# Computing only the 64 changed columns in each level of a triangular inverse, with level 0 turned by transposes

## Chip, cores and metric

The program runs on one core of one Trainium2 chip, written directly against the engines: TensorE (PE; its weight loads are shown apart as PEld), VectorE (DVE), ScalarE (ACT), GpSimd (POOL) and SyncE (SP, which only issues transfers). The metric is the device time of one execution in microseconds (us); lower is better.

## The reference

Three transformer blocks on one sequence of 256 tokens, width 1024, all in float32. The change lies in the first block, in its RWKV-7 mixer: 8 heads of width 64, with a recurrence over the tokens.

```python
def rwkv7_scan(r, w, k, v, a_vec, b_vec):
    def step(state, inp):
        rt, wt, kt, vt, at, bt = inp
        sa = jnp.einsum('bhvk,bhk->bhv', state, at)
        state = state * wt[:, :, None, :] + sa[..., None] * bt[:, :, None, :] + vt[..., None] * kt[:, :, None, :]
        return state, jnp.einsum('bhvk,bhk->bhv', state, rt)
    s0 = jnp.zeros((B, H, N, N), jnp.float32)
    _, y = lax.scan(step, s0, (tm(r), tm(w), tm(k), tm(v), tm(a_vec), tm(b_vec)))
    return y.transpose(1, 0, 2, 3)
```

The kernel doesn't step through the tokens. It cuts them into two chunks of 128. Within a chunk the terms `sa` solve a triangular system of 128 unknowns per head, so for each of the 16 pairs of chunk and head it forms a strictly triangular 128x128 matrix A and builds the inverse of (1 - A).

## The kernel before

**The inverse.** The 16 matrices stand side by side in `AAB` (128 partitions, 16 x 128 columns) and are worked in four groups `g` of four. There are seven levels `lv`. Level `lv` joins diagonal blocks of 2^lv rows to blocks of twice the size: a mask `lvl{lv}` picks from A the blocks that connect the halves of each pair (into `ALA`, by POOL). `TI` and `TJ` hold the inverse so far and its transpose. With level 0 both are set up (unit matrix plus the masked part). Each later level makes three products of 128x128 matrices for each of the 16 matrices:

- P = ALA^T TI (line 1091), which ACT copies from the accumulator to SBUF, tile `PP` (line 1118);
- J = PP^T TJ (line 1102), which DVE adds to `TJ` (line 1152);
- I = TJ^T PP (line 1109), which DVE adds to `TI` (line 1150; not in level 6).

Level 0 has one product, with the unit matrix as moving operand, which only turns `ALA` over (line 1091 too; lines 1141 and 1143 are DVE's two operations behind it). A float32 product is two instructions of PE in the trace, so 16 products are 32 rows of MATMUL. A transpose in PE's transpose mode (line 462) is one.

**Order.** PE runs a level as: P for groups 0 to 3, then for each group J and I. The groups' other work (POOL's mask, ACT's copy, DVE's additions) goes on beside it. Every engine has its own program in a fixed order. `wait_ge(*at(step))` waits for a named step of another engine, `up(...)` signals one, `bank(e, use)` takes one of the eight accumulator banks (`ps`) in turn and waits until its last use is freed.

**Around it.** Before the inverse PE makes the matrices A (`pe_mats`, line 1055) while DVE masks them (`dve_mats`, line 1064, 64 operations). In levels 2 and 3 DVE also does four operations of `dve_bonus` (lines 1126 to 1134). Behind the inverse `pe_recurrences` goes on with the decays of the linear attention (line 1283), the first chunk's right sides (line 1165: 128x64 moving columns), and further products of 64 columns (lines 1181, 1190, 1193), some over only 64 partitions (lines 1170, 1196, 1328).

**Memory.** `PP` stands in an area (`mats + 4096`) that earlier holds weights of the input projections. `mats + 6144` belongs to the same area and isn't used by the inverse.

Of the kernel before, what the change touches and what calls it, by code (L numbers as in the profile page):

```python
# [187 lines left out]
def program(nc, a):  # L188
    ctx = ExitStack()
    with ctx:  # L190
# [456 lines left out]
        LA = SIG  # L647
        mats = ARENA - 8192
        AAB = place(mats, 16, 128)
        PP = place(mats + 4096, 16, 128)  # L650
        AAK = place(ee + 2048, 16, 128)
        ARB = place(ee + 4096, 16, 128)
        ARK = place(mats + 2048, 16, 128)
# [10 lines left out]
        def group(x, g):  # L664
            return x[:, 4 * g:4 * g + 4, :]
# [4 lines left out]
        def four(use):  # L670
            return ps(use).rearrange("p (s t) -> p s t", s=4)
# [393 lines left out]
                k.then_inc(*up("masked", use, ("free", use)))  # L1065


        def pool_inverse(e):
            for lv in range(7):
                for g in range(NG):  # L1070
                    if lv == 0:
                        e.wait_ge(*at(("m", 4 * g + 3)))
                        if g == 0:
                            e.wait_ge(*at(("bt", 3)))
                            e.wait_ge(*at(("la", 1)))
                    else:
                        e.wait_ge(*at(("p done", lv - 1, g)))
                        if lv == 1:
                            e.wait_ge(*at(("tj", 0, g)))
                    e.tensor_tensor(group(ALA, g), group(AAB, g), bc(f"lvl{lv}"), ALU.mult).then_inc(  # L1080
                        *up("level", ("al", lv, g)))

        def pe_inverse(e):
            for lv in range(7):
                for g in range(NG):
                    b = bank(e, ("p", lv, g))
                    e.wait_ge(*at(("al", lv, g)))
                    if lv > 0:
                        e.wait_ge(*at(("ti", lv - 1, g)))
                    for s in range(4):  # L1090
                        k = e.matmul(b[:, s * P:s * P + P], ALA[:, 4 * g + s, :],  # L1091
                                     ident if lv == 0 else TI[:, 4 * g + s, :], start=True, stop=True)
                    k.then_inc(*up("inverse", ("p done", lv, g), ("full", ("p", lv, g))))
                if lv == 0:
                    continue
                for g in range(NG):
                    b = bank(e, ("j", lv, g))
                    e.wait_ge(*at(("pp", lv, g)))
                    if g == NG - 1:
                        e.wait_ge(*at(("tj", lv - 1, g)))  # L1100
                    for s in range(4):
                        k = e.matmul(b[:, s * P:s * P + P], group(PP, g)[:, s, :], TJ[:, 4 * g + s, :],  # L1102
                                     start=True, stop=True)
                    if lv == 6:
                        k.then_inc(*up("inverse", ("full", ("j", lv, g))))
                        continue
                    b = bank(e, ("i", lv, g))
                    for s in range(4):
                        k = e.matmul(b[:, s * P:s * P + P], TJ[:, 4 * g + s, :], group(PP, g)[:, s, :],  # L1109
                                     start=True, stop=True)  # L1110
                    k.then_inc(*up("inverse", ("full", ("i", lv, g)), ("full", ("j", lv, g))))

        def act_inverse(e):
            for lv in range(1, 7):
                for g in range(NG):
                    e.wait_ge(*at(("full", ("p", lv, g))))
                    e.wait_ge(*at(("tj", lv - 1, g)))
                    e.activation(group(PP, g), four(("p", lv, g)), ACT.Copy).then_inc(
                        *up("levels", ("pp", lv, g), ("free", ("p", lv, g))))

        def dve_bonus(e, t):
            if t == 0:
# [13 lines left out]
        def dve_inverse(e):  # L1136
            for g in range(NG):
                if g == 0:
                    e.wait_ge(*at(("kb", 1)))
                e.wait_ge(*at(("full", ("p", 0, g))))  # L1140
                e.tensor_tensor(group(TI, g), four(("p", 0, g)), bc("ident"), ALU.add).then_inc(
                    *up("tij", ("ti", 0, g), ("free", ("p", 0, g))))
                e.tensor_tensor(group(TJ, g), group(ALA, g), bc("ident"), ALU.add).then_inc(*up("tij", ("tj", 0, g)))
            for lv in range(1, 7):
                if lv in (2, 3):
                    dve_bonus(e, lv - 2)
                for g in range(NG):
                    e.wait_ge(*at(("full", ("j", lv, g))))
                    if lv < 6:
                        e.tensor_tensor(flat(group(TI, g)), ps(("i", lv, g)), flat(group(TI, g)), ALU.add).then_inc(  # L1150
                            *up("tij", ("ti", lv, g), ("free", ("i", lv, g))))
                    e.tensor_tensor(flat(group(TJ, g)), ps(("j", lv, g)), flat(group(TJ, g)), ALU.add).then_inc(
                        *up("tij", ("tj", lv, g), ("free", ("j", lv, g))))


        def pe_chunk(e, step):
# [1243 lines left out]
```

## Time and profile before

| | |
|---|---|
| median of 3 runs | 1299.88 us (1299.66 to 1301.49) |
| the profiled execution's own time | 1296.61 us |
| its span, from first to last instruction | 1294.6 us |
| PE / PEld busy | 1168.1 us (90%) / 1015.6 us (78%) |
| DVE / ACT / POOL busy | 749.6 / 524.1 / 120.8 us |
| TensorE clock granted, mean over the span | 0.905 of full |

The profiled execution is 3.3 us below the median of the runs; 2.0 us of its own time lie outside the span. The granted clock has two levels in the trace, 1.0 (2.4 GHz) and 0.5 (1.2 GHz). A stretch with a value between holds some of both. Busy time of PE counts an instruction from its start to its modelled end, so it says how long PE was occupied and not how much it computed. The time that an instruction takes in a stream is read from start to start.

### The profile page before, as it was taken

To read this page: it belongs to the slowest core of one execution; us is meant where nothing else is said; L and a number is where in the kernel's file an instruction comes from. 1 tells how busy PE (TensorE), PEld (TensorE's weight loads), DVE (VectorE), ACT (ScalarE), POOL (GpSimd) and SP (SyncE) were. 2 spreads that over 40 slices of the span, in tenths; PEclk is the share of its full clock that TensorE was granted. 3 is DMA by queue.
4 is the path that set the end of the run, shared out by engine and by line. 5 is a ranking of instruction groups with operands and counts; after the bars stand their busy time and mean duration, and the time that the engine had idled before them with its cause. 6 is when DMAs were issued, how large, how long until landed. Compare 5 with 4: busy or idle time off the path is not lost.

```text
span 1294.6 us, 17496 instructions
## 1 busy us (share of the span) xinstructions
PE 1168.1 (90%) x7196; PEld 1015.6 (78%) x7196; DVE 749.6 (58%) x1126; ACT 524.1 (40%) x742; POOL 120.8 (9%) x115
## 2 busy tenths in 40 slices
PE   5989799988799999779897993999699996999998
PEld 5788699876799988567666993998597555999885
DVE  3475685356676675746766742765653445666443
ACT  4443322023444343425664332443354344655331
POOL 0004354120300000300004000000100000000000
PEclk9899799768799999889997996999899568999999
DMA  9244000014587686234213889877253004565540
GB/s 287 85 150 153 1 2 1 1 33 163 186 269 261 228 288 240 99 122 155 98 34 121 302 165 278 274 261 262 94 170 124 0 2 130 163 195 180 205 169 32
DMA packets 112271, 193.69 MB, mean 150 GB/s; under 512 B 4514, under 2 KB 84913, under 8 KB 112066
## 3 DMA queue, kind: packets, MB, share of 16 engines
q1 hardware_dynamic: 108530, 179.65, 41.5%
q0 software_dynamic: 3248, 11.83, 4.1%
q8 instruction: 57, 0.93, 0.3%
q10 hardware_dynamic: 416, 1.11, 0.2%
q14 instruction: 20, 0.16, 0.0%
HBM read 188.38 MB, written 4.19 MB: 149 GB/s over the span
## 4 chain that ended last, share of the span: by engine, by line
PE 81%; DVE 9%; ACT 4%; DMA 3%; issue 2%; SPq 1%; POOL 0%; ACTq 0%; DVEq 0%
PE ps L399 20%; PE ps L400 20%; PE ps L401 20%; PE ps L1862 3%; PE ps L1845 3%; DMA ring<-in_ffn_w_gate_up_dram 3%; PE ps L1091 2%; PE ps L1837 2%; PE ps L1102 2%; DVE XL L532 1%; PE ps L1109 1%; DVE ARR L383 1%; PE ps L1328 1%; DVE AR L1064 1%; DVE STAT L549 1%
## 5 line engine op out<-in xcount | busy, mean ns | idle before, releaser
L383 DVE TENSOR_TENSOR ARR<-ring,ARR 128x2048 fp32r<-128x2048 f32 (+1 forms) x147 | 329.4, 2247 | 237.7 <-ACT ARR L372 237.5
L399 PE MATMUL ps<-XH,ARR 128*128 128x256 f32 x1232 | 355.8, 289 | 40.7 <-DVE ARR L383 21.0
L372 ACT ACTIVATE ARR<-ring 128x2048 fp32r<-128x2048 f32 (+1 forms) x147 | 274.8, 1877 | 249.3 <-PE ps L401 163.3
L400 PE MATMUL ps<-XL,ARR 128*128 128x256 f32 x1232 | 352.9, 286 | 0.0
L401 PE MATMUL ps<-XH,ARR 128*128 128x256 f32 x1232 | 352.5, 286 | 0.0
L399 PEld LDWEIGHTS ps<-XH,ARR 128*128 128x128 f32 x1232 | 239.4, 194 | 45.3 <-issue 38.9
L400 PEld LDWEIGHTS ps<-XL,ARR 128*128 128x128 f32 x1232 | 239.7, 195 | 0.0
L401 PEld LDWEIGHTS ps<-XH,ARR 128*128 128x128 f32 x1232 | 239.3, 194 | 0.0
L399 PE MATMUL ps<-ARR 128*128 128x512 f32 x388 | 157.3, 406 | 9.4 <-DVE ARR L484 5.8
L400 PE MATMUL ps<-ARR 128*128 128x512 f32 x388 | 155.4, 401 | 0.0
L401 PE MATMUL ps<-ARR 128*128 128x512 f32 x388 | 155.1, 400 | 0.0
L399 PEld LDWEIGHTS ps<-ARR 128*128 128x128 f32 x388 | 74.4, 192 | 31.0 <-DVE ARR L383 7.8
L401 PEld LDWEIGHTS ps<-ARR 128*128 128x128 f32 x388 | 74.4, 192 | 17.8
L400 PEld LDWEIGHTS ps<-ARR 128*128 128x128 f32 x388 | 74.5, 192 | 17.6 <-issue 0.5
L399 PE MATMUL ps<-ARR,XH 128*128 128x512 f32 (+1 forms) x160 | 62.4, 390 | 5.3 <-DVE XL L532 3.8
L400 PE MATMUL ps<-ARR,XH 128*128 128x512 f32 (+1 forms) x160 | 61.9, 387 | 0.0
L401 PE MATMUL ps<-ARR,XL 128*128 128x512 f32 (+1 forms) x160 | 61.6, 385 | 0.0
L1506 DVE SCALAR_TENSOR_TENSOR AR<-ring,AR 128x1024 f32<-128x1024 f32 x42 | 53.9, 1283 | 1.2
L592 POOL TENSOR_TENSOR X<-XN,GB 128x1024 f32<-128x1024 f32 x6 | 14.1, 2347 | 384.4 <-ACT XN L570 384.4
L462 PE MATMUL ps<-CST,XN 128*128 128x128 f32 x96 | 18.2, 352 | 31.1 <-ACT XN L2034 19.0
L1862 PE MATMUL ps<-AR 128*64 128x128 f32 x192 | 45.1, 357 | 1.0 <-ACT AR L1890 0.6
L1596 ACT ACTIVATE ARR<-XN 128x512 fp32r<-128x512 f32 x22 | 13.9, 633 | 74.6 <-DVE XN L1614 74.6
(333 smaller groups left out, 1432.4 us busy)
## 6 DMA issues: line engine op xcount, KB each, us to landing
ring<-in_ffn_w_gate_up_dram SPq DMA_DIRECT2D x44, 1024.0 KB, 5.9
ring<-in_w_dram SPq DMA_DIRECT2D x32, 1024.0 KB, 5.2
ring<-in_w_ada_dram SPq DMA_DIRECT2D x24, 1024.0 KB, 5.4
ring<-in_ffn_w_down_dram SPq DMA_DIRECT2D x22, 1024.0 KB, 5.1
ring<-in_even_w_in_dram SPq DMA_DIRECT2D x13, 1024.0 KB, 5.9
ring<-in_w_in_dram SPq DMA_DIRECT2D x9, 1024.0 KB, 5.3
ring<-in_mla_w_q_b_dram SPq DMA_DIRECT2D x6, 768.0 KB, 4.7
ring<-in_even_w_out_dram SPq DMA_DIRECT2D x4, 1024.0 KB, 4.8
```

The costliest lines, as they stand in the source:

```text
L372: e.activation(split(i)[0], raw(i), ACT.Copy).then_inc(*up("hi", ("hi", i)))
L383: e.tensor_tensor(lo, raw(i), hi.bitcast(F32), ALU.subtract).then_inc(*up("lo", ("lo", i), ("raw free", i)))
L399: e.matmul(out, lhs[0], rhs[0], start=first, stop=False)
L400: e.matmul(out, lhs[0], rhs[1], start=False, stop=False)
L401: return e.matmul(out, lhs[1], rhs[0], start=False, stop=last)
L462: k = e.transpose(ps((tag, c // 2))[:, o:o + P], src[:, t, c * P:(c + 1) * P], ident)
L1091: k = e.matmul(b[:, s * P:s * P + P], ALA[:, 4 * g + s, :], ident if lv == 0 else TI[:, 4 * g + s, :], start=True, stop=True)
L1102: k = e.matmul(b[:, s * P:s * P + P], group(PP, g)[:, s, :], TJ[:, 4 * g + s, :], start=True, stop=True)
L1506: k = e.scalar_tensor_tensor(acc, w[:, c, :], CSL[:, k0 + c:k0 + c + 1], acc, ALU.mult, ALU.add)
L1837: k = e.transpose(b[:, j * P:j * P + P], ex[:, j * P:j * P + P], ident)
L1845: e.matmul(b[:, 0:nk], A.q_of(h, t), A.k_of(h, nk), start=True, stop=True).then_inc(*up("scores", ("full", (A.tag, "score", i)), ("scored" ...
L1862: k = e.matmul(ps((A.tag, "o", g))[64 * (h % 2):64 * (h % 2) + 64, o:o + P], A.v_of(h, j), px[:, j * P:j * P + P], start=j == 0, stop=j == t)
```

## The change

For levels 1 to 6 the three products and the additions work on the 64 of 128 columns that the level changes. Those are every second block of 2^lv columns: `side(x, lv, which)` is a strided view of them. P is multiplied with the 64 columns of `TI` (side 0) and written to accumulator columns side by side; ACT spreads it into side 0 of `PP`. J takes the 64 columns of `TJ` (side 1), I the 64 columns of `PP` (side 0), and both share one bank, `("ji", lv, g)`. The weights (stationary operands) stay 128x128. As they read all of `PP`, its side 1 must be zero: there are two buffers `PPS` in turn, POOL clears both once (2048 columns each), and from level 3 on ACT clears side 1 of the next level's buffer by multiplying with 0. In level 0 the turn is a transpose.

```diff
-        PP = place(mats + 4096, 16, 128)
+        PPS = [place(mats + 4096 + 2048 * i, 16, 128) for i in range(2)]
+        PP = PPS[0]
...
+        def side(x, lv, which):
+            return x.rearrange("p s (b w t) -> p s b w t", w=2, t=1 << lv)[:, :, :, which, :]
+
+        def side_of(x, s, lv, which):
+            return x[:, s, :].rearrange("p (b w t) -> p b w t", w=2, t=1 << lv)[:, :, which, :]
+
+        def narrow(use, half, lv):
+            return ps(use)[:, 256 * half:256 * half + 256].rearrange("p (s b t) -> p s b t", s=4, t=1 << lv)
+
         def pool_inverse(e):
+            for b in range(2):
+                if b == 0:
+                    e.wait_ge(*now("pool_op"))
+                    e.wait_ge(*at(("used", weights[n_gate - 1])))
+                e.memset(PPS[b], 0.0).then_inc(*up("pp_clear", ("pp clear", b)))
...
                     for s in range(4):
-                        k = e.matmul(b[:, s * P:s * P + P], ALA[:, 4 * g + s, :],
-                                     ident if lv == 0 else TI[:, 4 * g + s, :], start=True, stop=True)
+                        if lv == 0:
+                            k = e.transpose(b[:, s * P:s * P + P], ALA[:, 4 * g + s, :], ident)
+                        else:
+                            k = e.matmul(b[:, 64 * s:64 * s + 64].rearrange("p (b t) -> p b t", t=1 << lv),
+                                         ALA[:, 4 * g + s, :], side_of(TI, 4 * g + s, lv, 0), start=True, stop=True)
...
+                pp = PPS[lv % 2]
                 for g in range(NG):
-                    b = bank(e, ("j", lv, g))
+                    b = bank(e, ("ji", lv, g))
                     e.wait_ge(*at(("pp", lv, g)))
+                    if lv > 2:
+                        e.wait_ge(*at(("pp zero", lv, g)))
+                    elif g == 0:
+                        e.wait_ge(*at(("pp clear", lv % 2)))
...
                     for s in range(4):
-                        k = e.matmul(b[:, s * P:s * P + P], group(PP, g)[:, s, :], TJ[:, 4 * g + s, :],
-                                     start=True, stop=True)
-                    if lv == 6:
-                        k.then_inc(*up("inverse", ("full", ("j", lv, g))))
-                        continue
-                    b = bank(e, ("i", lv, g))
-                    for s in range(4):
-                        k = e.matmul(b[:, s * P:s * P + P], TJ[:, 4 * g + s, :], group(PP, g)[:, s, :],
-                                     start=True, stop=True)
-                    k.then_inc(*up("inverse", ("full", ("i", lv, g)), ("full", ("j", lv, g))))
+                        k = e.matmul(b[:, 64 * s:64 * s + 64].rearrange("p (b t) -> p b t", t=1 << lv),
+                                     group(pp, g)[:, s, :], side_of(TJ, 4 * g + s, lv, 1), start=True, stop=True)
+                    if lv < 6:
+                        for s in range(4):
+                            k = e.matmul(b[:, 256 + 64 * s:320 + 64 * s].rearrange("p (b t) -> p b t", t=1 << lv),
+                                         TJ[:, 4 * g + s, :], side_of(pp, 4 * g + s, lv, 0), start=True, stop=True)
+                    k.then_inc(*up("inverse", ("full", ("ji", lv, g))))
...
                     e.wait_ge(*at(("full", ("p", lv, g))))
-                    e.wait_ge(*at(("tj", lv - 1, g)))
-                    e.activation(group(PP, g), four(("p", lv, g)), ACT.Copy).then_inc(
+                    if lv < 3:
+                        e.wait_ge(*at(("pp clear", lv % 2)))
+                    else:
+                        e.wait_ge(*at(("full", ("ji", lv - 2, g))))
+                    e.activation(side(group(pp, g), lv, 0), narrow(("p", lv, g), 0, lv), ACT.Copy).then_inc(
                         *up("levels", ("pp", lv, g), ("free", ("p", lv, g))))
+                if 2 <= lv < 6:
+                    for g in range(NG):
+                        e.wait_ge(*at(("full", ("ji", lv - 1, g))))
+                        e.activation(side(group(PPS[(lv + 1) % 2], g), lv + 1, 1), side(bc("ident"), lv + 1, 1),
+                                     ACT.Copy, scale=0.0).then_inc(*up("levels", ("pp zero", lv + 1, g)))
...
-                    e.tensor_tensor(flat(group(TJ, g)), ps(("j", lv, g)), flat(group(TJ, g)), ALU.add).then_inc(
-                        *up("tij", ("tj", lv, g), ("free", ("j", lv, g))))
+                    x = side(group(TJ, g), lv, 1)
+                    e.tensor_tensor(x, narrow(use, 0, lv), x, ALU.add).then_inc(*up("tij", ("tj", lv, g), ("free", use)))
```

The order in which PE's instructions stand doesn't move. This is PE's order before, from the last product of `pe_mats` to the middle of level 1 (here a float32 product is one entry; `AR` is the arena that holds all the matrices, `CST` the constants with the unit matrix):

```order
L1055 MATMUL ps<-GB,AR 128x256 x32
L1091 MATMUL ps<-CST,AR 128x128 x16
L1091 MATMUL ps<-AR 128x128 x16
L1102 MATMUL ps<-AR 128x128 x4
L1109 MATMUL ps<-AR 128x128 x4
```

And the same place after the change:

```order
L1056 MATMUL ps<-GB,AR 128x256 x32
L1108 MATMUL ps<-CST,AR 128x128 x16
L1110 MATMUL ps<-AR 128x64 x16
L1126 MATMUL ps<-AR 128x64 x4
L1130 MATMUL ps<-AR 128x64 x4
```

The number of products is the same, 16 + 6 x 32 + 5 x 16 = 288; the 272 of levels 1 to 6 have 64 columns in place of 128.

On ACT, one entry of 24 copies before:

```order
L1118 ACTIVATE AR<-ps 128x512 x24
```

becomes, after the change, 24 copies of 256 columns with 16 clearing operations between them:

```order
L1143 ACTIVATE AR<-ps 128x128x2 x4
L1143 ACTIVATE AR<-ps 128x64x4 x4
L1148 ACTIVATE AR<-CST 128x32x8 x4
L1143 ACTIVATE AR<-ps 128x32x8 x4
L1148 ACTIVATE AR<-CST 128x16x16 x4
```

The clearing for level `lv` + 1 stands behind the four copies of level `lv`.

## Rows read from the trace of the kernel before

**Rows 1.** Page: TensorE's granted clock, in tenths, in 40 slices of 32.4 us.

```profile
PEclk9899799768799999889997996999899568999999
```

**Rows 2.** Stretches: us; busy PE, PEld, DVE, ACT, POOL; clock, DMA, GB/s.

```profile
147.90:153.50 5.60, 3.15 (x25) 2.80 (x24) 5.60 (x28) 0.00 (x0) 1.80 (x3) 0.98 0.00 0
153.50:160.30 6.80, 5.74 (x24) 5.34 (x24) 6.80 (x8) 0.60 (x1) 4.73 (x4) 0.51 0.00 0
160.30:163.20 2.90, 2.05 (x16) 1.83 (x16) 0.56 (x1) 1.20 (x2) 2.21 (x3) 1.00 0.01 3
163.20:220.40 57.20, 57.20 (x515) 57.20 (x514) 39.24 (x51) 13.85 (x22) 26.51 (x20) 1.00 0.01 2
220.40:239.40 19.00, 19.00 (x171) 18.28 (x170) 11.41 (x17) 3.76 (x7) 8.93 (x5) 1.00 0.00 1
239.40:242.20 2.80, 2.00 (x13) 1.59 (x12) 0.84 (x2) 0.00 (x0) 0.00 (x0) 0.98 0.00 0
242.20:283.20 41.00, 41.00 (x185) 36.69 (x186) 14.38 (x23) 6.71 (x9) 8.49 (x7) 0.50 0.00 1
```

**Rows 3.** Groups by line, 163.2 to 220.4 us: busy, mean ns, idle before.

```profile
L1080 POOL TENSOR_TENSOR AR<-AR,CST 128x512 f32<-128x512 f32 x20 | 27.5, 1406 | 19.0 <-PE ps L1091 19.0
L1102 PE MATMUL ps<-AR 128*128 128x128 f32 x192 | 24.9, 275 | 0.0
...
L1150 DVE TENSOR_TENSOR AR<-ps,AR 128x512 f32<-128x512 f32 x20 | 13.7, 686 | 16.5 <-PE ps L1109 16.5
L1118 ACT ACTIVATE AR<-ps 128x512 f32<-128x512 f32 x21 | 12.6, 598 | 43.0 <-PE ps L1091 43.0
```

**Rows 4.** Timeline of PE, 216 to 232 us: start, length, instruction, count.

```profile
216.93 3.74 PE L1102 MATMUL ps<-AR 128*128 128x128 f32 x32
220.50 1.95 PE L1283 MATMUL ps<-CST,AR 128*128 128x128 f32 x16
222.29 1.90 PE L1165 MATMUL ps<-AR 128*128 128x64 f32 x16
224.03 1.11 PE L1283 MATMUL ps<-CST,AR 128*128 128x128 f32 x8
```

**Rows 5.** Timeline of PE, 253 to 284 us.

```profile
253.76 3.67 PE L1181 MATMUL ps<-AR 128*128 128x64 f32 x16
257.23 2.02 PE L1283 MATMUL ps<-CST,AR 128*128 128x128 f32 x8
259.18 3.09 PE L1328 MATMUL ps<-AR 64*128 64x128 f32 x16
...
277.48 6.12 PE L1328 MATMUL ps<-AR 64*128 64x128 f32 x45
```

**Rows 6.** Chain of waits, 262 to 263 us: start, length, line, instructions.

```profile
262.89 0.43 PE ps L1193 x2
```

**Rows 7.** Timeline of all engines, 127 to 163 us, parts.

```profile
127.37 0.84 PE L998 MATMUL ps<-AR 128*128 128x8 f32 x7
...
143.65 1.27 POOL L1080 TENSOR_TENSOR AR<-AR,CST 128x512 f32<-128x512 f32 x1 [19.66 <-DVE AR L1064]
146.81 1.27 POOL L1080 TENSOR_TENSOR AR<-AR,CST 128x512 f32<-128x512 f32 x1 [1.90 <-DVE AR L1064]
...
156.47 5.06 PE L1091 MATMUL ps<-AR 128*128 128x128 f32 x24
...
161.00 6.18 POOL L1080 TENSOR_TENSOR AR<-AR,CST 128x512 f32<-128x512 f32 x5 [0.69 <-DVE AR L1143]
...
162.37 1.13 PE L1091 MATMUL ps<-AR 128*128 128x128 f32 x8 [0.83 <-issue]
```

**Rows 8.** Groups of the whole run: nearest forms of 256 columns, and POOL's clear.

```profile
L1234 ACT ACTIVATE XN<-ps 128x256 f32<-128x256 f32 x4 | 1.5, 384 | 13.3 <-PE ps L1196 8.9 <-PE ps L1193 4.4
...
L1213 DVE COPY AR<-ps 128x256 f32<-128x256 f32 x4 | 1.6, 417 | 7.9 <-PE ps L1170 7.9
...
L729 POOL MEMSET AR<- 96x512 f32 x1 | 0.5, 527 | 0.0
```

More of the change, by code:

```diff
@@ L1113, in act_inverse @@
+                    k.then_inc(*up("inverse", ("full", ("ji", lv, g))))
         def act_inverse(e):
             for lv in range(1, 7):
+                pp = PPS[lv % 2]
                 for g in range(NG):
                     e.wait_ge(*at(("full", ("p", lv, g))))
-                    e.wait_ge(*at(("tj", lv - 1, g)))
-                    e.activation(group(PP, g), four(("p", lv, g)), ACT.Copy).then_inc(
-                        *up("levels", ("pp", lv, g), ("free", ("p", lv, g))))
+                    if lv < 3:
[3 more added lines that the diff above has]
+                    e.activation(side(group(pp, g), lv, 0), narrow(("p", lv, g), 0, lv), ACT.Copy).then_inc(
+                        *up("levels", ("pp", lv, g), ("free", ("p", lv, g))))
@@ L1147, in dve_inverse @@
                 for g in range(NG):
-                    e.wait_ge(*at(("full", ("j", lv, g))))
+                    use = ("ji", lv, g)
+                    e.wait_ge(*at(("full", use)))
                     if lv < 6:
-                        e.tensor_tensor(flat(group(TI, g)), ps(("i", lv, g)), flat(group(TI, g)), ALU.add).then_inc(
-                            *up("tij", ("ti", lv, g), ("free", ("i", lv, g))))
-                    e.tensor_tensor(flat(group(TJ, g)), ps(("j", lv, g)), flat(group(TJ, g)), ALU.add).then_inc(
-                        *up("tij", ("tj", lv, g), ("free", ("j", lv, g))))
+                        x = side(group(TI, g), lv, 0)
+                        e.tensor_tensor(x, narrow(use, 1, lv), x, ALU.add).then_inc(*up("tij", ("ti", lv, g)))
+                    x = side(group(TJ, g), lv, 1)
+                    e.tensor_tensor(x, narrow(use, 0, lv), x, ALU.add).then_inc(*up("tij", ("tj", lv, g), ("free", use)))
         def pe_chunk(e, step):
```

## The prediction

> **What bounds the stage now.** I looked first at the page's clock row [rows 1]: the inverse lies in the sixth and seventh slice (162 to 227 us), where the clock is almost full, with a slice of 7 ahead of it and 7, 6 and 8 behind. Then the stretches around it [rows 2]. From 163.2 to 220.4 us PE is busy for all of its 57.2 us with 515 instructions, at clock 1.00, while DVE has 39.2 us of work, ACT 13.9 and POOL 26.5. The groups of that stretch [rows 3] say the same from the other side: PE idles for 0.0 us before line 1102 (1091 and 1109 read the same), and DVE, ACT and POOL wait for PE (16.5 before line 1150, 43.0 and 19.0 us). So from the first J (line 1102) to the end of level 6 the stage is a single stream of PE, and its length is the number of PE instructions times the time of one. Those are 512: the 32 products of J and I of level 1, 4 x 48 of levels 2 to 5, 32 of level 6, two instructions each. 57.2 / 512 = 0.112 us. Ahead of it, in level 0 and the P of level 1, DVE and POOL set the pace: the last P waits for POOL's mask, which starts at 161.00 for that group, and runs at 162.37 [rows 7].
>
> **Part 1: 64 columns, at the full clock.** Count and order of the products stay. What does one of 64 columns take? The trace has them with the same weights of 128x128: 16 instructions of line 1165 from 222.29 to 224.03, 0.109 us each; and for 128 columns 32 of line 1102 from 216.93 to 220.50, 0.112 us each [rows 4]. Halving the columns is worth 3 ns at most, 512 x 0.003 = 1.5 us, and at the low level nothing that I could read; I take 0. The weight loads remain and are as many and as wide as before, which fits: PEld is busy for all of the 57.2 us [rows 2]. The Trainium skill says otherwise at one place ("TensorE: Matmul & The Clock Gate", Step-by-step: what each phase is for), where throughput is purely the number of moving columns; by it the sum would be minus half of 57.2 us. The trace doesn't agree, with 0.109 against 0.112, and decides.
>
> **Part 2: which clock.** An instruction of 64 columns at the low level takes (257.23 - 253.76) / 16 = 0.217 us [rows 5], two of line 1193 together 0.43 [rows 6], and the whole mixed stretch from 242.2 to 283.2 us has 185 in 41.0 us, 0.222 each [rows 2]. So the level decides 512 x (0.217 - 0.112), and I ask on which level the new stream starts and whether it leaves it.
>
> It starts low. In the kernel before the clock is low from 153.5 to 160.3 us (0.51) [rows 2], behind 5.6 us in which PE has 25 instructions and waits in between for DVE's masks. DVE still makes those 64 operations after the change; PE gets less to do there (16 transposes for 32 instructions in level 0). So the fall stays.
>
> Does it rise? Before, it rises at 160.3 us, and what PE did ahead of that was P of level 1, 128 columns wide and almost back to back from 156.47 [rows 7]. Those are now 64 columns wide, still handed out at DVE's pace. For 64 columns at the low level the trace has one long witness: 242.2 to 283.2 us, PE busy for all 41.0 us, clock 0.50 throughout [rows 2]. In it run lines 1165, 1181, 1190 and 1193 with 64 columns, and even 1181 followed without a gap by 1283 with 128 (253.76 to 259.18) didn't lift it [rows 5]. It rises only in the long run of line 1328 with 128 columns, 45 instructions from 277.48, that ends that stretch [rows 5]. On the other hand the 64 columns of line 1165 at 222.29 hold the high level when they start on it (clock 1.00 up to 239.4) [rows 2, 4]. I read this as: such a stream keeps the level that it finds. It finds the low one, so the 512 run at 1.2 GHz. I take 0.215 for one, as line 1193 has it, nearest in form (128x128 weights, 64 columns). 512 x 0.215 = 110.1 us for 57.2, **+52.9 us**.
>
> **Part 3: the edges.** The last P of level 1 (8 instructions, at the full clock from 162.37 to 163.2 before) take 8 x 0.215 = 1.7 for 0.8: **+0.9**. Behind the inverse line 1283 runs 16 instructions of 128 columns, from 220.50 to 222.29 before [rows 4]. They are what I expect to lift the clock, as line 1091 did at 160.3, but first run low: about 3.5 us for 1.8, **+1.7**. From there on the program is the old one, later, with its own low stretch as before, for the wait and the mixed products ahead of it (239.4 to 242.2 us, 13 instructions) are untouched.
>
> **Part 4: what is hidden.** Level 0: transposes in place of products. PE waits there for DVE and POOL (POOL idles 1.90 us for DVE ahead of its second mask [rows 7]), so this is 0; without that cover it would be 16 instructions, 1.8 us, less. POOL's two clears of 2048 columns: the nearest below is 0.527 us for 512 columns of 96 partitions [rows 8], so 2.1 us each; the nearest above POOL's own arithmetic, 1.27 us for 512 columns [rows 7], 5.1 each. They wait for the last use of the input weights; the first instruction behind that is line 998 at 127.37. Even 10.2 us end by 138, and POOL idles up to 143.65 [rows 7]: 0. Were that cover gone, the mask of level 0 would be late by what sticks out. ACT: copies of 256 columns, nearest 0.384 us (0.598 before), and 16 clears of which the trace has no row; between 0.384 and 0.598 each [rows 3, 8]. A level then has at most 8 x 0.6 = 4.8 us of ACT in 20.6 of PE. They stand behind the level's copies, 32 PE instructions ahead of the next level's, so nobody waits. DVE's additions halve (nearest 0.417 for 0.68 [rows 3, 8]) and stay hidden. A shared bank needs one free bank for two. All 0. Whether strided columns are read slower isn't in the trace for runs of 2 to 32 elements: from below nothing; from above a doubled read would still lie within or near the weight load at the low level, so I give it 0 and up to 10 us of range.
>
> **Sum.** 1296.6 + 52.9 + 0.9 + 1.7 = 1352 us for the profiled execution. That one lay 3.3 us under the median, so the median of the changed kernel is **1355 us**, 4.3% slower. What a measurement of this kernel tells from no change is about 0.2%, 2.6 us.
>
> **Rivals.**
> 1. *The clock recovers early in the inverse, no change.* For it: the stream is unbroken, and before the change an unbroken stream did lift the clock at 160.3. Against it: 41 us unbroken at 0.50 [rows 2]. Price: if it rises within the first few us, 0 to +4 us, 1299 to 1304. This one ends on the other side (not slower): it decides if the level is above 0.5 before some 10 of the 512 instructions are done. Each 10 instructions later cost 1.1 us. The Trainium skill speaks for it: the same page (Why this matters for your kernels) advises to keep TensorE busy without a gap to get and hold the full rate. By that rule 57 us without a gap would be at full rate and the time about 1300; the 41 us of rows 2 don't agree with it. Chance 8%.
> 2. *The first line behind the inverse doesn't lift the clock.* Then the 19.0 us from 220.4 to 239.4, 171 instructions [rows 2], run at 0.222 each, 38.0 us, and the low stretch joins the old one: +53.8 + 19.0, 1373 us. For it: line 1283 with 8 instructions didn't lift it at 257.23 [rows 5]. Against: here there are 16 in a row. Chance 8%.
> 3. *Columns do count*, and the clock is high: -28.6 + 0, 1271 us. Against it are rows 4. Chance 2%.
> 4. *My forecast*, as worked out above: 82%.
>
> **How the numbers follow.** 1355 is the fourth's. Its own range is 1349 to 1362: an instruction of 0.212 (the 0.43 may be 0.425) to 0.222 gives -1.5 to +4 us, the place of the rise behind the inverse about 2 us either way, the level of one execution against another 2 to 3 us. The common range goes from 1347 to 1374 and so takes in strided reads and rival 2; it leaves out rivals 1 and 3 and the tails, some 15%. Faster by over 0.2%: rival 3 and a sliver of 1, 0.03. Within 0.2%: most of rival 1, 0.06. Slower: 0.91.
>
> **What would show it.** Right: clock 0.50 in every stretch from about 153 to 273 us; 512 instructions of the three product lines at 0.212 to 0.217 us from start to start, DVE, ACT and POOL with more idle time before them than now, all for PE; first 1283 at about 273; clock 1.00 shortly behind it; the second low stretch again some 41 us long, from about 296. Part 1 is wrong if an instruction of 64 columns at clock 1.00 takes much less than 0.109 us. Part 4 is wrong if PE's product lines show idle time whose releaser is ACT or POOL. The forecast as a whole is wrong if the slices of the inverse show 9 in the clock row.

## The result: slower by 4.0%

The changed kernel takes 1352.5 us (median of 4 runs, 1351.29 to 1355.65), the kernel before beside it 1300.35 us (1299.66 to 1301.49). The ratio is 1.0404, 95% interval 1.0384 to 1.0423: 52.2 us more. The profiled execution took 1352.18 us, its span is 1350.2 us, 55.6 more than that of before.

The page of the changed kernel: busy time by engine, and the granted clock in 40 slices, here of 33.8 us. They answer to the table of before and to [rows 1].

```profile
PE 1223.4 (91%) x7180; PEld 1069.7 (79%) x7180; DVE 734.8 (54%) x1126; ACT 523.5 (39%) x758; POOL 123.0 (9%) x117
...
PEclk9899655585879999987999798899979559899999
```

PE has 16 instructions fewer than before and is busy for 55 us more. Its share rises from 90 to 91%, which looks like a kernel that uses its engine better. The clock row says what happened: the fifth to ninth slices (135 to 304 us) read 6, 5, 5, 5, 8, where before the slices of the inverse were nearly full.

The stretches of the changed kernel, with the columns of [rows 2]: end of the masks, P of level 1, the 512 instructions, the first products behind the inverse, and the two stretches that follow.

```profile
147.90:155.20 7.30, 2.02 (x9) 1.31 (x9) 7.30 (x24) 0.00 (x0) 3.79 (x3) 0.66 0.00 0
155.20:162.80 7.60, 7.54 (x32) 7.07 (x33) 4.36 (x5) 1.21 (x3) 5.63 (x5) 0.50 0.00 1
162.80:272.00 109.20, 109.20 (x513) 109.20 (x514) 25.54 (x51) 14.22 (x38) 24.25 (x19) 0.50 0.00 1
272.00:276.80 4.80, 4.80 (x26) 4.80 (x25) 2.41 (x4) 1.20 (x2) 2.04 (x2) 0.52 0.00 0
276.80:297.20 20.40, 19.60 (x165) 18.22 (x164) 9.14 (x16) 2.56 (x5) 6.91 (x4) 1.00 0.00 1
297.20:334.80 37.60, 37.60 (x168) 33.71 (x169) 13.15 (x22) 6.71 (x9) 7.27 (x5) 0.50 0.00 0
```

The third line stands against the fourth of [rows 2]: the same number of PE instructions, 109.2 us for 57.2, at 0.50 for 1.00. DVE's busy time in it falls from 39.24 to 25.54 us, as the change meant, and buys nothing.

The timeline of PE in the changed kernel (line 1110 is P, 1126 J, 1130 I; 1314 was 1283, 1196 was 1165), against [rows 4, 7].

```profile
155.19 7.82 PE L1110 MATMUL ps<-AR 128*128 128x64 f32 x32 [0.82 <-issue]
162.81 1.91 PE L1126 MATMUL ps<-AR 128*128 128x64 f32 x8
164.51 1.91 PE L1130 MATMUL ps<-AR 128*128 128x64 f32 x8
...
265.20 7.04 PE L1126 MATMUL ps<-AR 128*128 128x64 f32 x32
272.03 3.73 PE L1314 MATMUL ps<-CST,AR 128*128 128x128 f32 x16
275.55 2.40 PE L1196 MATMUL ps<-AR 128*128 128x64 f32 x16
277.78 1.11 PE L1314 MATMUL ps<-CST,AR 128*128 128x128 f32 x8
```

From the first J at 162.81 to line 1314 at 272.03 are 109.22 us, 0.2133 us for each of 512. In the kernel before the first J stands at 163.33 and line 1283 at 220.50, 57.17 us apart:

```profile
163.33 1.06 PE L1102 MATMUL ps<-AR 128*128 128x128 f32 x8
```

In the changed kernel's stream there is no gap, and the eight instructions of a group take 1.71 us from start to start in every level.

The groups of the same stretch (162.8 to 272 us), and of the whole run POOL's clears in its timeline; they answer to [rows 3].

```profile
L1126 PE MATMUL ps<-AR 128*128 128x64 f32 x192 | 45.3, 420 | 0.0
...
L1096 POOL TENSOR_TENSOR AR<-AR,CST 128x512 f32<-128x512 f32 x19 | 24.9, 1315 | 59.2 <-PE ps L1110 59.2
...
L1182 DVE TENSOR_TENSOR AR<-ps,AR 128x256 f32<-128x256 f32 x20 | 8.5, 425 | 75.3 <-PE ps L1130 75.3
L1143 ACT ACTIVATE AR<-ps 128x256 f32<-128x256 f32 x21 | 8.1, 384 | 91.4 <-PE ps L1110 91.4
L1148 ACT ACTIVATE AR<-CST 128x256 f32<-128x256 f32 x16 | 5.3, 405 | 0.0
```

```profile
126.39 3.57 POOL L1084 MEMSET AR<- 128x2048 f32 x2 [3.68 <-PE ps L401]
```

Every other engine waits for PE: 59.2, 75.3 and 91.4 us where [rows 3] had 19.0, 16.5 and 43.0. PE waits for none of them.

**Where the 55.6 us arise.** I compared the starts of the same instructions in the two traces. The first J starts 0.5 us earlier (162.81 for 163.33). The 512 add 52.0, so line 1314 starts 51.5 later than line 1283 did. The 16 of it and the 16 narrow ones behind it take 5.75 us for 3.53, so the next group of that line is 53.8 later. The second low stretch is 37.6 us long for 41.0, and behind it the difference is 52.7. The last 3 us come later, in stages that the change doesn't touch, between 341 us and the end; the medians differ by 52.2, so I read these 3 us as the difference of one execution from another. The profiled execution of before itself lies 3.7 us under the median of 1300.35.

### The profile page after: what moved, and what is told of

Its sections match the earlier page's. It is cut to its first block, busy times and chain, and to the rows that moved or that the text cites. A ratio compares the mean times of both kernels' runs of the same rounds, so it can differ in the third digit from the quotient of the medians.

```text
span 1350.2 us, 17487 instructions
## 1 busy us (share of the span) xinstructions
PE 1223.4 (91%) x7180; PEld 1069.7 (79%) x7180; DVE 734.8 (54%) x1126; ACT 523.5 (39%) x758; POOL 123.0 (9%) x117
## 4 chain that ended last, share of the span: by engine, by line
PE 82%; DVE 9%; ACT 4%; DMA 3%; issue 2%; SPq 1%; POOL 0%; ACTq 0%; DVEq 0%
PE ps L399 19%; PE ps L400 19%; PE ps L401 19%; PE ps L1110 3%; PE ps L1126 3%; PE ps L1893 3%; PE ps L1876 3%; PE ps L1130 3%; DMA ring<-in_ffn_w_gate_up_dram 2%; PE ps L1868 2%; DVE XL L532 1%; DVE ARR L383 1%; PE ps L1359 1%; DVE AR L1065 1%; PE ps L1314 1%
## 5 line engine op out<-in xcount | busy, mean ns | idle before, releaser
L1537 DVE SCALAR_TENSOR_TENSOR AR<-ring,AR 128x1024 f32<-128x1024 f32 x42 | 53.9, 1283 | 1.2
L1143 ACT ACTIVATE AR<-ps 128x256 f32<-128x256 f32 x24 | 9.3, 386 | 113.1 <-PE ps L1110 113.1
L1182 DVE TENSOR_TENSOR AR<-ps,AR 128x256 f32<-128x256 f32 x20 | 8.5, 425 | 75.3 <-PE ps L1130 75.3
```

Source lines behind the costliest of these rows:

```text
L1537: k = e.scalar_tensor_tensor(acc, w[:, c, :], CSL[:, k0 + c:k0 + c + 1], acc, ALU.mult, ALU.add)
```

## The experiments

Medians of all runs of a kernel; the ratio is to the kernel before on the same chip, with its 95% interval.

| kernel | us | ratio |
|---|---|---|
| change, P of level 1 wide | 1298.05 (12 runs) | 0.9993, 0.9976 to 1.001 |
| change, P of level 3 wide | 1315.32 (4) | 1.0123, 1.0098 to 1.0148 |
| change, adjacent columns | 1357.17 (1) | |
| before, level 0 by transposes | 1299.47 (12) | 0.9993, 0.9978 to 1.0009 |
| change, weights in halves | 1270.59 (1), again 1274.77 (6) | 0.9819, 0.9792 to 0.9846 |
| before, weights in halves | 1297.77 (10) | 0.9993, 0.998 to 1.0005 |
| change, halves in another order | 1285.54 (1) | |
| before, second chunk paired | 1292.25 (10) | 0.9947, 0.9924 to 0.9969 |
| change, P of level 1 wide, paired | 1281.54 (6) | 0.9892, 0.9851 to 0.9933 |
| change, weights in halves, paired | 1265.57 (6) | 0.9733, 0.9708 to 0.9758 |

Line numbers below are those of each experiment's own program.

### 1. Is it only the level on which the stream starts?

P of level 1 gets its 128 columns back, and ACT copies half of them. All else stays: 512 narrow instructions follow.

```diff
+        WIDE_P = (1,)
...
+                        elif lv in WIDE_P:
+                            k = e.matmul(b[:, s * P:s * P + P], ALA[:, 4 * g + s, :], TI[:, 4 * g + s, :],
+                                         start=True, stop=True)
...
-                    e.activation(side(group(pp, g), lv, 0), narrow(("p", lv, g), 0, lv), ACT.Copy).then_inc(
+                    src = side(four(("p", lv, g)), lv, 0) if lv in WIDE_P else narrow(("p", lv, g), 0, lv)
+                    e.activation(side(group(pp, g), lv, 0), src, ACT.Copy).then_inc(
```

> The changed kernel, but the 16 P of level 1 alone are 128 columns wide again (ACT still copies only the 64 that change). Theory (the level of the clock): the 128-column P lift the clock at about 160 us as in the kernel before, and the 64-column stream behind them keeps the high level; the 512 instructions take 0.112 us each, the stretch from the first J to the end of level 6 about 57 us, the time 1298 to 1303 us. Rival (the narrow instructions themselves, their strides, or the changed work of ACT and DVE cost the time): 32 of 544 instructions are undone, so about 1349 us. Rival 2 (64 columns don't keep the high level): the clock falls again within the inverse, 1310 to 1350 us.

Measured: 1298.05 us. Stretches and timeline of PE of this kernel (1112 is the wide P, 1131 the J, 1320 the first line behind the inverse):

```profile
152.70:163.00 10.30, 7.22 (x32) 6.11 (x30) 9.19 (x16) 0.81 (x2) 6.04 (x5) 0.51 0.00 1
163.00:200.00 37.00, 36.86 (x331) 36.70 (x330) 20.70 (x34) 9.07 (x26) 23.31 (x17) 1.00 0.01 2
```

```profile
157.52 7.01 PE L1112 MATMUL ps<-AR 128*128 128x128 f32 x32 [0.82 <-issue]
164.36 1.00 PE L1131 MATMUL ps<-AR 128*128 128x64 f32 x8
...
221.48 0.78 PE L1320 MATMUL ps<-CST,AR 128*128 128x128 f32 x5
```

The clock rises within the wide P, as before the change, and the 512 narrow instructions keep it: 57.12 us from 164.36 to 221.48, 0.1116 each. The whole loss is gone with 32 instructions of 512 + 32 changed back, and no gain appears. Two things are shown: the level is the cause of the 52 us, and at the high level 64 columns are worth nothing beside 128 (0.1116 here; 57.2 / 512 = 0.1117 in the kernel before, [rows 2]).

### 2. Does a wide group further on lift it too?

The same edit with `WIDE_P = (3,)`.

> The changed kernel, but the 16 P of level 3 alone are 128 columns wide. Theory (the level of the clock): low until these P, which start at about 197 us, lift it within their 6.8 us; the 320 instructions behind them then take 0.112 instead of 0.213 us and give back 32 us and up to 2 more: 1316 to 1322 us. Rival (cost of the narrow instructions themselves): 1349 us.

Measured: 1315.32 us. Stretches, and timeline of PE around the wide P (line 1112):

```profile
160.00:200.00 40.00, 39.96 (x187) 39.64 (x187) 12.21 (x22) 3.96 (x11) 12.14 (x10) 0.50 0.01 1
200.00:210.00 10.00, 10.00 (x86) 10.00 (x86) 6.24 (x9) 2.75 (x8) 5.91 (x4) 0.94 0.00 0
```

```profile
198.38 5.18 PE L1112 MATMUL ps<-AR 128*128 128x128 f32 x32
203.39 1.00 PE L1131 MATMUL ps<-AR 128*128 128x64 f32 x8
```

The low level lasts until the wide P and ends inside it; after that J takes 0.11 us an instruction again. From 164.25 to 198.38 stand 160 narrow instructions at 0.2133 in place of 0.1116, 16.3 us; the measured loss is 16.0 us. The near agreement of the two is partly luck. Inside the inverse the trace shows more: line 1320, the first behind it, starts at 239.07 for 220.50, 18.6 us later. That is 16.3 for the 160, 0.9 for the later first J (164.25 for 163.33) and 1.4 for the wide P itself, which runs partly low (5.0 us for 32 x 0.1117 = 3.6). Behind the inverse this execution gets 10 us back, because its second low stretch is broken: the clock is 0.51 from 262.6 to 269.4 us, 0.99 up to 279.7 and 0.50 up to 289.9. So within the inverse the price is the number of narrow instructions ahead of the first wide group times 0.102 us and little besides; what reaches the end of the kernel also hangs on the second low stretch. The expectation (1316 to 1322) was missed by under 1 us.

### 3. Do strided columns cost anything?

`side_of` takes adjacent columns. The kernel leaves out the right choice of columns, so it computes another product of the same size.

```diff
-            return x[:, s, :].rearrange("p (b w t) -> p b w t", w=2, t=1 << lv)[:, :, which, :]
+            return x[:, s, 64 * which:64 * which + 64].rearrange("p (b t) -> p b t", t=1 << lv)
```

> The changed kernel, with PE's moving operands read as 64 columns side by side in place of every second block; this leaves out that they are the right columns. Theory: a strided read costs nothing, instruction 0.213 us, 1350 to 1355 us. Rival (strides make the stream slower, most in level 1 with runs of 2 elements): shorter by what the strides cost.

Measured: 1357.17 us in one run, span 1355.1. Timeline of PE, the J of level 6 and the line behind it:

```profile
267.30 7.04 PE L1126 MATMUL ps<-AR 128*128 128x64 f32 x32
274.13 3.73 PE L1314 MATMUL ps<-CST,AR 128*128 128x128 f32 x16
```

Its first J starts at 164.90, 2.1 us later than in the changed kernel, which is the 2 us over the expected range; the 512 take 109.23 us, as with strides. Strided moving operands cost nothing here, at runs of 2 to 32 columns. That was read at the low level and, in experiment 1, at the high one (0.1116). In both the time of an instruction hardly depends on its moving columns, so a small cost of the strides could hide. Experiment 5 closes that gap: there the columns count, and level 1 (runs of 2) takes 0.0294 us an instruction and level 5 (runs of 32) 0.0293.

### 4. Level 0 by transposes alone

The kernel before, with `e.transpose(...)` for the product in level 0 and nothing else.

> The kernel before with only level 0 changed to transposes, all else 128 columns wide. Theory: level 0 waits for DVE and POOL, and the wide P of level 1 lift the clock as before: within 2 us of 1300. Rival (16 fewer instructions ahead of level 1 cost or shift the rise of the clock): later rise, up to +4 us and more; or the 1.8 us less are a gain.

Measured: 1299.47 us, ratio 0.9993. Half the instructions in level 0 are worth nothing, because PE waits there for POOL's masks (line 1080), as its timeline shows:

```profile
152.07 1.09 PE L1092 MATMUL ps<-CST,AR 128*128 128x128 f32 x4 [2.36 <-POOL AR L1080]
155.23 1.09 PE L1092 MATMUL ps<-CST,AR 128*128 128x128 f32 x4 [2.07 <-POOL AR L1080]
```

The clock isn't disturbed by them either.

### 5. What bounds an instruction: the weights?

At the high level 64 and 128 moving columns take the same time, and PEld is busy throughout. If the load of 128 weight columns is that floor, a product cut into two with 64 weight columns each should get under it. The second half goes to output partitions 64 to 127, so the half changes with every second instruction of PE. Every product of levels 1 to 6 is made so; the computation stays whole.

```diff
+        def two(e, out, lv, lhs, rhs):
+            for h in range(2):
+                r = slice(64 * h, 64 * h + 64)
+                k = e.matmul(out[r, :].rearrange("p (b t) -> p b t", t=1 << lv), lhs[:, r], rhs, start=True, stop=True)
+            return k
```

> The changed kernel, with each product of levels 1 to 6 made as two of 64 weight columns (output partitions 0 to 63 and 64 to 127), 64 moving columns each: 1088 instructions in place of 544, the same result. Theory (the time of an instruction of 64 moving columns is that of its weight load of 128 columns): one of 64 weight columns takes about half, 0.11 us at the low level, and the sum stays near that of the changed kernel, 1345 to 1365 us; if the denser stream lifts the clock, down to about 1300. Rival (a fixed time for each instruction, whatever it loads): twice the stream, about 1460 us at the low level.

Measured: 1270.59 us, the first version that beats the kernel before, and outside both expectations: neither half the time of an instruction nor a fixed time. Timeline of PE (1082 are all split products, 1318 the first line behind the inverse), two stretches inside the inverse and four behind it:

```profile
161.26 11.32 PE L1082 MATMUL ps<-AR 128*64 128x64 f32 x336 [0.84 <-issue]
174.90 6.42 PE L1082 MATMUL ps<-AR 128*64 128x64 f32 x192 [2.31 <-DVE AR L1186]
183.31 17.07 PE L1082 MATMUL ps<-AR 128*64 128x64 f32 x512 [2.00 <-DVE AR L1186]
200.31 2.05 PE L1318 MATMUL ps<-CST,AR 128*128 128x128 f32 x16
```

```profile
184.80:188.00 3.20, 3.20 (x63) 3.20 (x64) 0.68 (x3) 2.01 (x7) 3.20 (x4) 0.50 0.02 5
188.00:200.30 12.30, 12.30 (x422) 12.24 (x419) 7.25 (x19) 5.83 (x14) 6.03 (x5) 1.00 0.02 5
...
222.20:232.40 10.20, 10.20 (x42) 8.70 (x41) 1.54 (x3) 0.60 (x1) 1.15 (x1) 0.50 0.01 2
232.40:242.60 10.20, 10.20 (x80) 9.17 (x79) 7.50 (x13) 2.45 (x4) 2.45 (x2) 1.00 0.00 0
242.60:252.80 10.20, 10.20 (x53) 9.27 (x53) 3.97 (x6) 3.55 (x4) 3.10 (x3) 0.50 0.01 2
252.80:263.00 10.20, 5.96 (x63) 5.57 (x61) 9.02 (x16) 3.07 (x3) 2.01 (x3) 1.00 0.33 103
```

And DVE's additions for three groups of level 5 (line 1186 takes I, once for every 32 instructions of PE):

```profile
194.82 0.42 DVE L1186 TENSOR_TENSOR AR<-ps,AR 128x256 f32<-128x256 f32 x1 [0.18 <-PE ps L1082]
...
195.75 0.42 DVE L1186 TENSOR_TENSOR AR<-ps,AR 128x256 f32<-128x256 f32 x1 [0.18 <-PE ps L1082]
...
196.69 0.42 DVE L1186 TENSOR_TENSOR AR<-ps,AR 128x256 f32<-128x256 f32 x1 [0.18 <-PE ps L1082]
```

Twice as many instructions, and the inverse ends at 200.31 for 220.50. The 512 of the third line take 17.0 us, 0.0332 each, but 3.2 us of that are at the low level. At clock 1.00 a group of 32 takes 0.935 us, 0.0292 for one, and 422 in 12.3 us say the same. So a product, now four instructions, takes 0.117 us where its two took 0.223. DVE is now waited for behind levels 2 and 3 (2.31 and 2.00 us), where it has the four `dve_bonus` operations: a cover that the old stream gave and this one doesn't. The narrow stream also lifts the clock by itself: the mean over 163 to 200.3 us is 0.94, though P of level 1 is narrow too. It doesn't hold it throughout: 1.5 us behind the second of the two waits the clock falls to 0.50, from 184.8 to 188.0 us. Of the span's 26.1 us less 20.2 are the inverse; the rest lies behind it, where 41 us at 0.50 have become 10 us at 0.50, 10 at 1.00 and 10 at 0.50, with 1.00 behind them. Why they do is not settled; the work in them is the same.

Run again:

> The change with split weights once more, for an interval: 1270.6 in the one run, against 1299 to 1300 for before, so a ratio near 0.978. If the one run was a lucky one, it lies nearer 1280.

Measured: 1274.77 us, 6 runs, ratio 0.9819, between the two expectations. The one run before had been on the low side. The clock falls inside the inverse here too, from 185.8 to 189.2 us, again behind the two waits.

### 6. Is it the short weights, the narrow columns, or the side by side?

First the kernel before with all its 128 moving columns and only the weights in halves (`two` without the strides).

> The kernel before, all 128 moving columns kept, but each product of levels 1 to 6 made as two with 64 weight columns each, to output partitions 0 to 63 and 64 to 127. 1024 split instructions pairs where before has 512 times two. Theory A (in the change's narrow form with split weights the 0.034 us per instruction came from short weight columns alone, whatever the moving columns are): the stretch is about as short as in that run, some 37 us between 163 and the first decay product instead of 57, and the time is near that run's 1270. Theory B (once the weight load is no floor, the moving columns count): 128 columns cost up to twice what 64 cost, 1024 x 0.068 = 70 us if fully so, at least the 57 of before; the time is then 1300 to 1315. Between them, 0.05 us each (51 us) would give 1294. The mean gap from start to start of these instructions decides.

Measured: 1297.77 us. Timeline of PE:

```profile
162.98 56.99 PE L1071 MATMUL ps<-AR 128*64 128x128 f32 x1040 [0.86 <-issue]
219.90 2.05 PE L1289 MATMUL ps<-CST,AR 128*128 128x128 f32 x16
```

1040 in 56.92 us are 0.0547 each, at clock 1.00: twice as many at half the time (0.109 us for the two in place of 0.112), no gain in the median. So neither edit is worth anything alone, and together they are worth 20 us. With 128 weight columns the columns of the moving operand don't count (0.1116 for 0.1117); with 64 they do (0.0292 for 0.0547, both at clock 1.00). Theory B of this expectation held in what it says of the columns; the time is 2 us under its range, at the low end of its count. The rule of the Trainium skill ("TensorE: Matmul & The Clock Gate", Step-by-step: what each phase is for) that throughput is purely the number of moving columns would give, as an estimate from the page, 0.053 us for 128 at 2.4 GHz and 0.027 for 64. The first agrees with the 0.0547 of the halved weights, the second is a little under their 0.0292, and with whole weights neither holds.

Then the change with split weights, but half 0 of four products ahead of half 1 of the same four, so that the half changes with every eighth instruction in place of every second. The diff is against experiment 5, cut to J.

```diff
+        EIGHT = [(s, h) for h in range(2) for s in range(4)]
...
-                    for s in range(4):
-                        k = two(e, b[:, 64 * s:64 * s + 64], lv, group(pp, g)[:, s, :], side_of(TJ, 4 * g + s, lv, 1))
+                    for s, hh in EIGHT:
+                        k = two(e, b[:, 64 * s:64 * s + 64], lv, group(pp, g)[:, s, :], side_of(TJ, 4 * g + s, lv, 1), hh)
```

> The change with split weights, but the eight instructions of a product group in another order: first half 0 of four products, then half 1 of four. Same instructions, same operands. Theory A (0.034 us each comes from the weight load of 64 columns instead of 128, and nothing else): the gap stays 0.034, the time 1270. Theory B (two neighbours that use different halves of the output partitions run side by side, and it is that which brings 0.109 to 0.034): neighbours now mostly share a half, the gap goes to some 0.055 (half of 0.109), the stretch grows by 1024 x 0.02 = 21 us and the time is near 1291. In both the clock must be looked at: if it stays at the low level, the gap is twice as long.

Measured: 1285.54 us in one run. Timeline of PE, and the stretch of its 512:

```profile
185.91 19.04 PE L1084 MATMUL ps<-AR 128*64 128x64 f32 x512 [0.85 <-DVE AR L1189]
204.88 2.05 PE L1321 MATMUL ps<-CST,AR 128*128 128x128 f32 x16
```

```profile
185.91:204.88 18.97, 18.97 (x513) 18.90 (x513) 9.48 (x26) 8.35 (x21) 9.96 (x8) 1.00 0.01 3
```

0.0371 us each. This stretch is at clock 1.00 throughout, so it stands against 0.0292 and not against the 0.0332 that held a low stretch: the frequent change of half is worth a fifth, not the factor of three to four. Theory A is nearer in mechanism, but its "nothing else" fell. What stays open is why 64 weight columns bring an instruction of 64 moving columns from 0.1116 to 0.029, a quarter (0.037 in this order), and not just to half. A load that takes half as long for half the columns would leave 0.056. The run is 10.8 us over the repeated one of experiment 5, but only 3.3 of them are the inverse (204.88 for 201.55 in that trace, which has 3.4 us at the low level where this one has none). The rest lies behind it: here the clock is 0.50 from 227.0 to 268.1 us, 41 us as in the kernel before. So the part of the gain that stands in the inverse is the split's, 19 to 20 us, and what lies behind it depends on how the second low stretch falls out.

### 7. The second low stretch

It costs before and after alike. In it products over 64 partitions (upper or lower) follow one another; two banks filled in turn let an upper and a lower one stand next to each other. Cut to its core, for lines 1165 and 1170 (and in the same way for 1190, 1193, 1196):

```diff
+                for i in range(4):
+                    for j in range(2):
+                        h = 2 * i + j
+                        e.matmul(both[j][:, sl], AAK[:, 8 * t + h, :], VT[:, t, 64 * h:64 * h + 64],
+                                 start=True, stop=False)
...
+                    for j in range(2):
+                        r = slice(64 * j, 64 * j + 64)
+                        k = e.matmul(both[j][:, sl], CAR[r, i, t, 0, :], S0[r, i, :], start=False, stop=True)
```

> The kernel before; the inverse untouched. In the second chunk the products over 128 partitions and those over 64 (lines 1165 and 1170, and 1190, 1193, 1196) alternate no longer one by one: both halves of the heads in two banks, first the two of 128 partitions, then the two of 64. Theory (the level holds if PE streams more evenly): the low stretch behind the inverse, 242 to 283 us, doesn't begin or is shorter; up to 20 us less, 1280 to 1290 us. Rival (the level falls at the wait for the state at 239.5 us, whatever follows): the clock is low all the same and the order saves only the switches between the shapes, some 3 to 5 us.

Measured, the kernel before with it: 1292.25 us. Timeline of PE and the low stretch:

```profile
241.43 0.66 PE L1164 MATMUL ps<-AR 128*128 128x64 f32 x4
242.02 0.44 PE L1170 MATMUL ps<-AR,GB 64*128 64x64 f32 x4
```

```profile
244.10:274.80 30.70, 30.70 (x159) 28.52 (x160) 13.65 (x22) 6.60 (x9) 7.61 (x6) 0.50 0.00 1
```

Four instructions of line 1170 take 0.36 us from start to start where two did before, so the two on the other 64 partitions cost nothing beside them. Four of line 1164, over all 128 partitions, take 0.59 where two of 1165 took 0.36: those two more cost their full 0.11 each. Two heads together take 0.95 us for 1.46. The clock still falls, 2 us later, but 159 instructions remain in the low stretch for 185, and it is 30.7 us long for 41.0. The gain, 6.5 us, is under the theory's and a little over the rival's; the rival's premise, that the clock falls all the same, held.

> The changed kernel with the P of level 1 wide, and the second chunk paired as in the run on the kernel before. Theory: the sum of the two effects, that is the time of the paired kernel on the old inverse, within 2 us, since the narrow inverse at the high level is worth nothing on PE. Rival: the narrow inverse ends with the clock on another footing and loses the high level sooner, 10 us and more slower than the paired kernel on the old inverse.

Measured, the change with a wide P of level 1 and the pairs: 1281.54 us. That is 10.7 under the paired kernel before, though experiment 1 found no gain in the narrow form, and neither the theory nor the rival allowed for it. The profiled run has the low stretch exactly as above (30.7 us at 0.50); its own time, 1289.33, is also the second highest of the six. The mean granted clock of each run goes with its time: four of the six took 1277.4 to 1282.4 us at 0.912 to 0.915, the other two 1289.3 and 1295.6 us at 0.902 and 0.898; of the paired kernel before one of ten took 1280.05 us at 0.914 and nine took 1291.1 to 1294.9 at 0.899 to 0.908. So the medians differ by how often the clock was higher. In which stretch it was, no trace shows, for both profiled executions are of the lower clock, and whether the narrow inverse makes the higher one more frequent stays open.

> The change with split weights (1270.6 in one run) and the second chunk's products paired over two banks (which alone gave 1292.3 against 1299.5 of before). If the two gains add: 1270.6 - 7 = 1263 to 1264. If the second stretch at the low level in the split kernel no longer falls where the pairing helps, the pairing gives nothing: 1270. A loss is possible if the pairing delays the first bank's evictions: up to 1275.

Measured: 1265.57 us, ratio 0.9733, the fastest version. The gain over the split alone is 9.2 us, so the two gains add, within the scatter (6.5 us for the pairing alone). Timeline of PE:

```profile
176.65 6.76 PE L1082 MATMUL ps<-AR 128*64 128x64 f32 x192 [2.31 <-DVE AR L1186]
185.06 3.80 PE L1082 MATMUL ps<-AR 128*64 128x64 f32 x103 [1.65 <-DVE AR L1186]
```

The two waits for DVE are still there (the second is 1.65 us, and this execution keeps clock 1.00 behind it). They are some 4 us that moving `dve_bonus` out of levels 2 and 3 could try for, and with it the 3.2 us at the low level of experiment 5. It wasn't tried.

## Why the prediction was right, step by step

Forecast 1355 us in a range of 1347 to 1374, measured 1352.5.

- **Part 1, nothing for 64 columns**: right, and shown by experiment 1. The take came from 0.109 of line 1165; in the stream itself it is 0.1116.
- **Part 2, the stream starts low and stays low**: right. +52.9 forecast, +52.0 measured, with 0.2133 us for the 0.215 taken. That the missing wide P is the reason was an argument then; experiments 1 and 2 have shown it.
- **Part 3, the edges**: +0.9 for the last P was the right size: P of level 1 takes 7.6 us for 6.9, +0.8. The first J starts 0.5 us earlier all the same, because the whole execution is 1.3 us ahead before it comes to anything that was changed: POOL's small MEMSET stands at 120.67 for 121.95, and level 0 hands over at 155.19 for 156.47. That is scatter; in the trace of experiment 1 the same MEMSET stands at 123.01. Behind the inverse +2.2 for +1.7. The clock rose at 276.8, not within the 16 instructions of line 1314 but in the narrow ones behind them.
- **Part 4, hidden work**: right. POOL's clears took 1.8 us each at 126.4, under the lower bound of 2.1 worked out for them; ACT's copies 0.384 us, its clears (5.3 us for 16) 0.33 to 0.41, also at or under the low bound. Strides cost 0 (experiment 3), transposes brought 0 (experiment 4). The 10 us kept in the range for strides were not needed.
- **The second low stretch**: forecast as unchanged, it began at about 297 and is 3.4 us shorter, which gives back 1.1 us by the same instructions in both traces (53.8 ahead of it, 52.7 behind).
- **The sum**: 55.5 us forecast, 52.7 found up to there, 52.2 between the medians. The 2.8 us between the first two are the first J (1.4, nearly all of it the early start), the stream (0.9), the second stretch (1.1), less 0.5 at the edge. So the changed part itself came to 55.0 of the 55.5 forecast (52.0, 0.8 and 2.2). That the profiled execution took 1352.18 us as summed is chance: its 3 us of late scatter fill that gap.
- **Rival 1** (recovers early) didn't happen. The sentence of the Trainium skill that it rested on ("TensorE: Matmul & The Clock Gate", Why this matters for your kernels), to keep TensorE busy without gaps, isn't enough: PE is busy for all of the 109.2 us at 0.50. **Rival 2** didn't either: the clock did rise, if 1.3 us behind line 1314. **Rival 3**, columns count, is false for this form and true once the weights are halved: the prediction took the weight load as given and didn't ask what lies under that floor. One slip in rival 1: 10 instructions more at the low level cost 1.0 us, not 1.1.

## What to carry to other kernels

Before narrowing the moving operand, read two instructions of the old and the new width with the same weights from the trace: if they take the same time, the moving columns aren't what bounds them, and narrowing them alone pays nothing; here narrowing the weights as well paid 20 us, and either alone 0. Then ask what the wide instructions do for the clock: thirty-two of them at the head of a stream decided over 52 us, so with whole weights try one wide group where a stream starts at the low level, and judge PE by granted clock and busy time together, not by the busy share.

## What the runs showed of the hardware that was not expected

- The same narrow stream has two lasting states. Started at 0.50 it stays there for 109 us without a gap (0.2133 us each), started at 1.00 it stays at 1.00 (0.1116). A wide group of 32 moves it from the first to the second at level 1 and at level 3 alike.
- A stream of narrow instructions with halved weights leaves the low level by itself: in the repeated run its unbroken part starts at 162.70 us at 0.50, and the mean over 163 to 201 us is 0.92. It lost the level again for 3.4 us (185.8 to 189.2) behind two waits of 2.31 and 1.97 us for DVE.
- Halving weights and moving columns together brings an instruction from 0.1116 to 0.0292 us at clock 1.00, to a quarter, and so a product from 0.223 to 0.117; with the half changing at every eighth instruction it is 0.0371.
- The second low stretch isn't fixed in length. It is 41.0 us in the kernel before, 37.6 in the changed one, 30.7 when paired, and in experiments 2 and 5 it has some 10 us at 1.00 in its middle.
